# Two chained transformer blocks: the memory layer in two stages with one coefficient table, and a third weight slot for the experts

## The chip, the cores and the metric

One core of one Trainium2 chip runs the whole program in one launch. The metric is device microseconds (us) from the first to the last instruction of a run; lower is better. All data are 32-bit floats.

## The reference, cut to what matters

The program is one block of a first kind, then one of a second kind, on 512 tokens of width 1024. Two parts matter here. The first block ends in a mixture of experts: each token picks 2 of 32 experts, each with three weight matrices.

```python
def expert_block(args):
    xb, e = args
    hid = jax.nn.silu(xb @ w_gate[e]) * (xb @ w_up[e])
    return hid @ w_down[e]
```

The second block has a large memory of 16384 entries (128 x 128 keys), each with a row u and a row v of 1024 numbers. Each token ranks the keys under 8 heads, takes 16 entries per head (128 in all), and sums their v rows, each weighted by its gate and by the gelu of the token's product with u.

```python
v1, i1 = lax.top_k(s1, PEER_TOPK)
v2, i2 = lax.top_k(s2, PEER_TOPK)
...
top, pos = lax.top_k(cand, PEER_TOPK)
...
a = jax.nn.gelu(jnp.einsum('td,thkd->thk', xc, u_tab[ec]), approximate=False)
return jnp.einsum('thk,thkd->td', gc * a, v_tab[ec])
```

## The kernel before, in words

Each stage is a block of five instruction streams (SP and POOL issue DMAs, PE multiplies matrices, ACT and DVE do the rest), written out by hand and tied by semaphores; all engines meet at a stage's end. Weights of ordinary products stream through a ring of two 2 MB halves, `wring`, filled on SP's queue up to two blocks ahead (`load_blocks`, L114).

**Experts** (`stage_router` L1184, `stage_experts` L1358). The router ranks the tokens and builds the row lists. Its SP stream loads eight small tables, then fills the result table `y_dram` in DRAM with 12.6 MB (L1219), because the experts later scatter only used rows into it. The experts run as 24 blocks; a block holds 2 experts of 64 rows each. Of every 6 expert places, 4 are fixed experts and 2 are overflow places, loaded only when used (`cond`, L1432). A block needs 4 MB of gate and up weights (`ex_gu`, two slots) and 2 MB of down weights (`ex_dn`, two slots). On PE the order is: gate and up of block b+1 (L1483), transposes of the hidden rows of b (L1490), transposes of the rows of b+2 (L1473), down of b (L1501). A gate and up slot is refilled when the block two before has used it.

**Retention core** (`stage_ret_core` L942). Its first work on every engine is a decay product on DVE (L986) that waits for two tables, `rc_kdec` and `rc_band`, loaded at the head of its SP stream (L969, L970); PE's first product (L1044) waits for it.

**Memory** (`stage_memory_route` L2037, `stage_memory` L2283). Tokens 256 to 511 (two tiles of 128) are done densely: for each of the 128 blocks of 128 entries, PE multiplies the block of u (0.5 MB) with the tokens, ACT takes the gelu (scores), DVE multiplies by the tokens' coefficients for that block (`weigh`, L2496), and PE multiplies by the block of v (0.5 MB) (outputs, L2394). The coefficients come from one-hot matrices: for 8 tokens DVE compares twice and multiplies once (L2482, L2484, L2487), PE multiplies the two matrices (L2386), and ACT keeps the result (L2445). The table is built in 4 parts of 32 columns, so each group of 8 tokens is done 4 times. Tokens 0 to 255 are done by gathers: POOL issues one indirect DMA per token tile and slot (128 rows of 4 KB, 0.5 MB) into a ring of 8; DVE makes one product and sum per u gather (L2509) and one multiply and add per v gather (L2563).

The route stage ranks 4 token tiles on DVE (47 us each) while PE does the queries, the key scores and the first 32 of the 128 score blocks, whose gelu goes to DRAM (`g_dram`); one of the ranking's products is on POOL (L2092). The memory stage then has a build of the first part of the coefficients (with the u gathers of tile 0 beside it) and four passes of 32 blocks. In the passes stand beside the outputs: the rest of the u gathers of tile 0 and the build of part 2; the v gathers of tile 0, scores, and the build of part 3; the u gathers of tile 1, scores, and part 4; the v gathers of tile 1 and scores.

Of the kernel before, what the change touches and what calls it, by code (L numbers as in the profile page):

```python
# [11 lines left out]

# [38 lines left out]
class Env:  # L51


    def __init__(self, nc, ctx, dram):
# [7 lines left out]
        self.shared = {}  # L62
        self.chained = 0

# [49 lines left out]
def load_blocks(env, sp, ahead=2, until=None):  # L114

    nc = env.nc
    for b in range(env.issued, min(env.used + ahead, len(env.blocks)) if until is None else until):
# [24 lines left out]
class Group:  # L142
# [5 lines left out]
    def __call__(self, eng, steps):  # L148
# [3 lines left out]
        eng.wait_ge(self.sem, self.env.chained)  # L152
# [789 lines left out]
def stage_ret_core(env, R, oT):  # L942
# [9 lines left out]
    with ExitStack() as stk:  # L952
# [226 lines left out]
TRIPLES = LATER // 2  # L1179
UNUSED = 8192.0  # L1180
# [3 lines left out]
def stage_router(env, E):  # L1184
# [6 lines left out]
    with ExitStack() as st:  # L1191
# [19 lines left out]
        with nc.Block() as block:  # L1211
            @block.sync
            def _(sp):
# [3 lines left out]
                for dst, name in loads:  # L1217
                    nc.sync.dma_start(dst[:], dram[name]).then_inc(in_s, 16)
                nc.sync.dma_start(dram["y_dram"].rearrange("(b p) d -> p b d", p=P),  # L1219
                                  env.gates[:, 0, :].unsqueeze(1).broadcast_to([P, NB, D])).then_inc(E.y_set, 16)  # L1220
# [137 lines left out]
def stage_experts(env, E):  # L1358
# [7 lines left out]
    x_got, gu_got, dn_got, y_out = ([env.sem(f"ex_{n}{s}") for s in range(SLOT)]  # L1366
                                    for n in ("x_got", "gu_got", "dn_got", "y_out"))
    gain, shift = (lambda j: env.gain[:, 2, j:j + 1]), (lambda j: env.ada[:, 24 + j, 0:1])
    ROWS, GU, HID, DOWN = [0, 1], [2, 3], 5, [6, 7]
    with ExitStack() as st:  # L1370
# [5 lines left out]
        gu, dn = T("gu", [P, SLOT, 2, GUW]), T("dn", [P, SLOT, 2, EFT * D])  # L1376
        silu, hid, hidT = T("silu", [P, SLOT, EF]), T("hid", [P, SLOT, EF]), T("hidT", [P, SLOT, EFT, P])
        wg = [[gu[:, s, h, :].rearrange("p (k n) -> p k n", k=KD) for h in range(2)] for s in range(SLOT)]
        wd = [[dn[:, s, h, :].rearrange("p (k n) -> p k n", k=EFT) for h in range(2)] for s in range(SLOT)]
# [6 lines left out]
        with nc.Block() as block:  # L1386
            @block.gpsimd
            def _(pool):
# [22 lines left out]
                pool.wait_ge(E.y_set, 16)  # L1411
# [12 lines left out]
            def _(sp):  # L1424
# [3 lines left out]
                def load(part, who, lo, n, s, got, rows=None):  # L1428
                    for h in range(2):
                        src = dram["experts"][bass.ds(who[h], 1), :, lo:lo + n].rearrange("o p n -> p (o n)")  # L1430
                        if rows is not None and rows[h] is not None:
                            nc.sync.dma_start(part[:, s, h, :], src, cond=rows[h]).then_inc(got[s], 16)  # L1432
                        else:
                            nc.sync.dma_start(part[:, s, h, :], src).then_inc(got[s], 16)

                def replace(g, n):

                    b = 3 * g + n
# [1473 lines left out]
```

## Time and profile before

| | us |
|---|---|
| median of 3 runs (3399.39 to 3406.08) | 3400.16 |
| the profiled execution, its own time | 3413.92 |
| its span, first to last instruction | 3412.1 |
| experts, first gate and up product to last down product | 1133.3 to 1483.2 |
| route stage and memory stage, first rank to last gather product | 1993.9 to 3319.8 |

Busy shares of the span: PE 89%, PEld (weight loads) 53%, DVE 47%, ACT 15%, POOL 22%. TensorE's granted clock averages 0.916 of full speed. Traffic is 668.5 MB, of which 281 MB are gathers and scatters. A span's time in a window is read as busy microseconds per engine; a DMA share near 1 means that the 16 DMA engines had packets all the time.

### The profile page before, as it was taken

Reading aid. Unit: us, or ns where it says so; the run is one execution under the profiler, and the core shown is the slowest. Engines: PE = TensorE matmul, PEld = TensorE weight load, DVE = VectorE, ACT = ScalarE, POOL = GpSimd, SP = SyncE. Lnnn points to the kernel's source line nnn. Section 1 sums busy time; section 2 is a strip of 40 time slices with the busy share of each in tenths; the row PEclk is TensorE's granted clock in tenths of the full one; section 3 lists DMA queues with packets and bytes.
Section 4 is the critical chain, followed back from the end, with each engine's and each line's share of the span. In section 5 each row is a group of like instructions: output and inputs, shape, how many; then the busy total and the mean of one; then the engine's idle time right before and its main releaser. Section 6 shows DMA issues by size and latency. Waiting matters only on the chain. (4 is left out here: it accounts for less than half of the span.)

```text
span 3412.1 us, 35969 instructions
## 1 busy us (share of the span) xinstructions
PE 3021.8 (89%) x11616; PEld 1798.3 (53%) x11616; DVE 1616.1 (47%) x3314; ACT 504.0 (15%) x1079; POOL 758.9 (22%) x688
## 2 busy tenths in 40 slices
PE   6988999988986688859888899598899999999987
PEld 3436444445434223324445487495567777776553
DVE  1135100113012212232056169988888888886772
ACT  2223100011001011131146121010000000000002
POOL 0000000000000111110000001345565556556650
PEclk8898998999997799979999899658899999999998
DMA  5010341020115888841200125358999999999992
GB/s 202 37 51 1 148 153 66 35 96 25 74 74 226 344 346 326 318 154 57 105 13 1 50 70 160 132 154 299 326 351 381 366 344 382 362 361 377 410 359 102
DMA packets 156365, 668.54 MB, mean 196 GB/s; under 512 B 22131, under 2 KB 31731, under 8 KB 140915
## 3 DMA queue, kind: packets, MB, share of 16 engines
q1 hardware_dynamic: 73684, 383.16, 29.5%
q0 software_dynamic: 81792, 281.07, 22.2%
q10 hardware_dynamic: 800, 3.15, 0.2%
q8 instruction: 53, 0.87, 0.1%
q14 instruction: 36, 0.29, 0.0%
HBM read 689.31 MB, written 35.65 MB: 212 GB/s over the span
## 5 line engine op out<-in xcount | busy, mean ns | idle before, releaser
L2394 PE MATMUL ps<-wring,pm_weighted 128*128 128x512 f32 x1024 | 488.5, 622 | 41.5 <-DVE pm_weighted L2496 41.4
L414 PE MATMUL ps<-hT,wring 128*128 128x512 f32 (+2 forms) x1232 | 467.3, 541 | 16.4 <-PEq L573 4.9
L414 PEld LDWEIGHTS ps<-hT,wring 128*128 128x128 f32 (+1 forms) x1232 | 233.6, 191 | 247.0 <-issue 238.8
L2368 POOL DMA_INDIRECT pm_ring<-in_peer_u,pm_idxs x256 | 316.4, 1236 | 195.8 <-DVE pm_dots L2509 116.0
L2377 PE MATMUL ps<-hT,wring 128*128 128x256 f32 x1536 | 352.7, 383 | 0.0
L2563 DVE SCALAR_TENSOR_TENSOR gates<-pm_ring,pm_coefs,gates 128x1024 f32<-128x1024 f32 x256 | 316.7, 1280 | 61.1 <-DMA pm_ring<-in_peer_v,pm_idxs 60.9
L2368 POOL DMA_INDIRECT pm_ring<-in_peer_v,pm_idxs x256 | 303.3, 1185 | 139.0 <-issue 57.1
L2394 PEld LDWEIGHTS ps<-wring,pm_weighted 128*128 128x128 f32 x1024 | 197.8, 198 | 255.5 <-issue 196.9
L2386 PEld LDWEIGHTS ps<-pm_onehot,hT 128*128 128x128 f32 x2048 | 294.0, 226 | 49.5 <-issue 49.5
L2377 PEld LDWEIGHTS ps<-hT,wring 128*128 128x128 f32 x1536 | 286.8, 190 | 49.4 <-issue 14.4
L2509 DVE CUSTOM_DVE_ANT_0 pm_ring<-pm_ring,mem_x 128x1024 f32<-128x1024 f32 x256 | 300.5, 1219 | 2.3 <-DMA pm_ring<-in_peer_u,pm_idxs 2.3
L1393 POOL COPY ex_idx<-row_token 128x1 uint32 (+1 forms) x24 | 4.4, 185 | 1304.5 <-PEq L1506 1116.7
L2386 PE MATMUL ps<-pm_onehot,hT 128*128 128x32 f32 x2048 | 286.7, 302 | 2.1 <-DVE pm_onehot L2487 2.1
L1483 PE MATMUL ps<-ex_gu,hT 128*64 128x512 f32 x768 | 187.1, 644 | 49.5 <-DMA ex_gu<-in_experts 47.5
L937 PE MATMUL ps<-wring,hT 128*128 128x512 f32 (+1 forms) x544 | 213.9, 555 | 1.2 <-PEq L362 1.2
L1562 DVE TENSOR_SCALAR hT<-ps,gain,ada 128x128 f32<-128x128 f32 x192 | 63.4, 401 | 278.4 <-PE ps L1473 278.4
L2092 POOL TENSOR_TENSOR pk_eq<-pk_eq,pk_ixf 128x2048 f32<-128x2048 f32 x4 | 26.0, 6488 | 647.2 <-DVE pk_eq L2086 647.2
L937 PEld LDWEIGHTS ps<-wring,hT 128*128 128x128 f32 x544 | 98.4, 190 | 116.2 <-issue 116.2
L2484 DVE TENSOR_TENSOR hT<-pm_iota,pm_keyT 128x1024 f32<-128x1024 f32 x128 | 155.9, 1218 | 0.0
L1483 PEld LDWEIGHTS ps<-ex_gu,hT 128*64 128x64 f32 x768 | 58.7, 148 | 175.7 <-issue 172.2
L2445 ACT ACTIVATE pm_coef_part<-ps 128x256 f32 x128 | 49.2, 384 | 623.8 <-PE ps L2386 623.8
L2496 DVE TENSOR_TENSOR pm_weighted<-pm_weighted,pm_coef_part 128x256 f32<-128x256 f32 x128 | 76.6, 598 | 122.3 <-ACT pm_weighted L2439 82.9
(422 smaller groups left out, 3147.1 us busy)
## 6 DMA issues: line engine op xcount, KB each, us to landing
ex_gu<-in_experts SPq DMA_DIRECT2D x48, 2048.0 KB
wring<-in_peer_v SPq DMA_DIRECT2D x128, 512.0 KB, 7.6
ex_dn<-in_experts SPq DMA_DIRECT2D x48, 1024.0 KB
wring<-in_peer_uT SPq DMA_DIRECT2D x96, 512.0 KB, 5.6
wring<-in_w_in SPq DMA_DIRECT2D x21, 2048.0 KB, 7.7
ada_w<-in_w_ada SPq DMA_DIRECT2D x12, 2048.0 KB, 10.9
pk_u<-in_peer_uT SPq DMA_DIRECT2D x32, 512.0 KB, 3.8
y_dram_out<-gates SPq DMA_DIRECT2D x1, 12288.0 KB, 33.6
```

Source lines behind the costliest of these rows:

```text
L414: mm = env.nc.tensor.matmul(out, w[:, k, lo:hi], rhs(k), start=(k == 0), stop=(k == KD - 1))
L937: mm = env.nc.tensor.matmul(env.ps[:, t[0], 0:n], env.hT[:, k, i * P:(i + 1) * P], w[:, k, lo:lo + n], start=(k == 0), stop=(k == KD - 1))
L1483: mm = nc.tensor.matmul(env.ps[r, GU[s], :], xT[:, s, k, r], wg[s][h][:, k, :], start=(k == 0), stop=(k == KD - 1))
L1562: nc.vector.tensor_scalar(xT[:, s, k, :], env.ps[:, ROWS[n], j * P:(j + 1) * P], gain(k), shift(k), ALU.mult, ALU.add).then_inc(xT_done, 1)
L2368: nc.gpsimd.indirect_dma_start(ring[:, r, :], None, dram[table], bass.IndirectOffsetOnAxis(ap=idx[:, half, r:r + 1], axis=0)).then_inc(got ...
L2377: mm = nc.tensor.matmul(env.ps[:, SCORE[s % 2], 0:DS], uT[s][:, k * P:(k + 1) * P], env.hT[:, k, GT * P:S], start=(k == 0), stop=(k == KD ...
L2386: mm = nc.tensor.matmul(env.ps[:, CB[s % 2], j * PB:(j + 1) * PB], A(s % 2)[:, j, :], B[:, s % 2, j, :], start=True, stop=True)
L2394: mm = nc.tensor.matmul(env.ps[:, OUT[n], :], W[:, s % 2, t * P:(t + 1) * P], vr[s][:, half * WBLK:(half + 1) * WBLK], start=False, stop=stop)
L2484: nc.vector.tensor_tensor(A(s % 2), iota[:].unsqueeze(1).broadcast_to([P, GRP, PK]), keyT[:, 0, ts].unsqueeze(2).broadcast_to([P, GRP, PK] ...
L2496: nc.vector.tensor_tensor(W[:, s % 2, :], W[:, s % 2, :], C[:, part % 2, :, bass.ds(n, 1)].rearrange("p t o -> p (t o)"), ALU.mult).then_i ...
L2509: nc.vector.tensor_tensor_reduce(ring[:, r, :], ring[:, r, :], xg[:, t, :], 1.0, 0.0, ALU.mult, ALU.add, dots[:, n:n + 1]).then_inc(used, 1)
L2563: nc.vector.scalar_tensor_tensor(acc[:, n % 2, :], ring[:, r, :], coef[:, bass.ds(i * PER + n, 1)], acc[:, n % 2, :], ALU.mult, ALU.add).t ...
```

## The change: what it does

1. **Memory, first stage** (`stage_memory_scores`): all 128 score blocks move here, loaded four at a time (2 MB, three buffers: one own, two in `wring`) and stored four at a time. The u gathers of both tiles move here too: as soon as tile 0 is ranked, POOL issues them, and DVE does two products (`FILL`) after the last instruction of each group of the ranking, before it waits for the group. The rest follow after the ranking. The one product that POOL did goes to DVE.
2. **Memory, second stage** (`stage_memory_outputs`): first one table of coefficients `C` [128, 256 tokens, 128 columns] is built on chip, 32 groups of 8 tokens once each, 128 columns wide. Then 128 output blocks, with v in pairs (1 MB), the stored gelu in fours (0.5 MB), and two v gathers a block; the products of the gathers are added straight into `h`. Until the table is done only 3 of the 8 gather buffers are used.
3. **Experts**: a third gate and up slot in `wring`. The weights of the experts that are fixed are loaded in the router stage already: all of block 0, one half of block 1, and one gate and up half of block 2. `wring` is refilled for the second block after the last expert product only.
4. The 12.6 MB fill of `y_dram` moves from the router stage to the head of the retention core's SP stream, ahead of `rc_kdec` and `rc_band`.

```diff
@@ stage_ret_core
             @block.sync
             def _(sp):
+                nc.sync.dma_start(env.dram["y_dram"].rearrange("(b p) d -> p b d", p=P),
+                                  env.gates[:, 0, :].unsqueeze(1).broadcast_to([P, NB, D])).then_inc(env.y_set, 16)
                 nc.sync.dma_start(kdec[:], dram["ret_kdec"]).then_inc(in_s, 16)
@@ stage_router
-                nc.sync.dma_start(env.dram["y_dram"]...).then_inc(E.y_set, 16)
+                for h in range(2):
+                    nc.sync.dma_start(E.gu[0][h], dram["experts"][h, :, 0:GUW]).then_inc(E.gu_got[0], 16)
+                for h in range(2):
+                    nc.sync.dma_start(E.dn[0][h], dram["experts"][h, :, GUW:]).then_inc(E.dn_got[0], 16)
+                for n, h in ((1, 0), (2, 1)):
+                    nc.sync.dma_start(E.gu[n][h], dram["experts"][n + 1, :, 0:GUW]).then_inc(E.gu_got[n], 16)
+                    if n == 1:
+                        nc.sync.dma_start(E.dn[n][h], dram["experts"][n + 1, :, GUW:]).then_inc(E.dn_got[n], 16)
@@ stage_experts, SP
+                def gate_up(i, n):
+                    sp.wait_ge(gu_full, ROUND * i + n - GUS + 1)
+                    load(i, n, E.gu, 0, GUW, gu_got)
+                def down(i, n):
+                    sp.wait_ge(dn_full, 2 * (ROUND * i + n - SLOT) + 2)
+                    load(i, n, E.dn, GUW, GUW + EFT * D, dn_got)
...
@@ stage_memory_scores
+                for n in range(GT * SLOTS):
+                    if n % SLOTS == 0:
+                        pool.wait_ge(rows_s, n // SLOTS + 1)
+                    if n >= RING:
+                        pool.wait_ge(G.used, n - RING + 1)
+                    nc.gpsimd.indirect_dma_start(ring[:, n % RING, :], None, dram["peer_u"], ...)
+                for n in range(QUADS):
+                    if n >= UBUF:
+                        product_done(env, sp, u_t[QUAD * (n - UBUF) + QUAD - 1])
+                    nc.sync.dma_start(u[n % UBUF], dram["peer_uT"][n]).then_inc(u_in[n % UBUF], 16)
+                    if n >= UBUF:
+                        store(n - UBUF)
@@ stage_memory_outputs, DVE
+                with v.Fori(0, groups // 2) as i:
+                    for q in range(2):
+                        v.wait_ge(c_full, n + 1)
+                        nc.vector.tensor_tensor(B[q], iota..., keyT[:, 1, ts]..., ALU.is_equal)
+                        nc.vector.tensor_tensor(A[q], iota..., keyT[:, 0, ts]..., ALU.is_equal)
+                        nc.vector.tensor_tensor(B[q], B[q], keyT[:, 2, ts]..., ALU.mult)
+                v.wait_ge(c_done, 4 + 2 * groups)
+                        for j in range(QUAD):
+                            nc.vector.tensor_tensor(here, here, C[:, :, bass.ds(m, 1)]..., ALU.mult)
+                            for r in (2 * j, 2 * j + 1):
+                                nc.vector.scalar_tensor_tensor(env.h[:, t, :], ring[r], coef..., env.h[:, t, :],
+                                                               ALU.mult, ALU.add)
```

## Rows read from the trace of the kernel before

**Rows 1.** The page, DMA in 40 slices: share of 16 engines, then GB/s

```profile
DMA  5010341020115888841200125358999999999992
GB/s 202 37 51 1 148 153 66 35 96 25 74 74 226 344 346 326 318 154 57 105 13 1 50 70 160 132 154 299 326 351 381 366 344 382 362 361 377 410 359 102
```

**Rows 2.** Windows of the memory: length, busy us by engine, granted clock, DMA share, GB/s

```profile
1990.00:2045.00 55.00, 55.00 (x315) 48.56 (x315) 50.35 (x240) 14.68 (x29) 6.49 (x1) 1.00 0.19 50
2188.00:2300.00 112.00, 109.86 (x515) 107.49 (x513) 97.43 (x164) 12.23 (x33) 63.28 (x43) 0.53 0.61 193
2529.00:2793.00 264.00, 264.00 (x1215) 192.40 (x1213) 225.06 (x251) 23.07 (x60) 157.86 (x140) 1.00 0.98 367
3110.00:3318.00 208.00, 194.59 (x651) 121.30 (x650) 151.90 (x140) 10.38 (x27) 137.78 (x119) 1.00 1.01 405
```

**Rows 3.** Groups by line, memory and route: busy us, mean ns | idle before

```profile
L2394 PE MATMUL ps<-wring,pm_weighted 128*128 128x512 f32 x1024 | 488.5, 622 | 41.5 <-DVE pm_weighted L2496 41.4
L2563 DVE SCALAR_TENSOR_TENSOR gates<-pm_ring,pm_coefs,gates 128x1024 f32<-128x1024 f32 x256 | 316.7, 1280 | 61.1 <-DMA pm_ring<-in_peer_v,pm_idxs 60.9
L2484 DVE TENSOR_TENSOR hT<-pm_iota,pm_keyT 128x1024 f32<-128x1024 f32 x128 | 155.9, 1218 | 0.0
L414 PE MATMUL ps<-hT,pk_u 128*128 128x256 f32 x512 | 113.7, 385 | 7.9 <-DMA pk_u<-in_peer_uT 7.9
L2496 DVE TENSOR_TENSOR pm_weighted<-pm_weighted,pm_coef_part 128x256 f32<-128x256 f32 x128 | 76.6, 598 | 122.3 <-ACT pm_weighted L2439 82.9 <-DMA wring<-in_peer_v 29.8 <-ACT pm_coef_part L2445 8.8
L2487 DVE TENSOR_TENSOR pm_onehot<-pm_onehot,pm_keyT 128x256 f32<-128x256 f32 x128 | 53.4, 417 | 0.0
```

**Rows 4.** Timeline of DVE around the first ranked tile, then a u-gather product

```profile
1993.93 3.20 DVE L2232 MAX8 pk_v<-pk_sc 128x8 f32<-128x128 f32 x16 [26.02 <-ACT pk_sc L2177]
2029.35 6.49 DVE L2092 TENSOR_TENSOR pk_eq<-pk_eq,pk_ixf 128x2048 f32<-128x2048 f32 x1
2040.72 0.23 DVE L2275 CAST mem_rows<-pk_pick 128x128 uint32<-128x128 f32 x1
2195.67 1.22 DVE L2509 CUSTOM_DVE_ANT_0 pm_ring<-pm_ring,mem_x 128x1024 f32<-128x1024 f32 x1
2196.82 0.42 DVE L2482 TENSOR_TENSOR pm_onehot<-pm_iota,pm_keyT 128x256 f32<-128x256 f32 x1
```

**Rows 5.** Timeline of PE in the experts, from a period of three blocks

```profile
1406.57 1.04 PE L1473 MATMUL ps<-ident,hT 128*128 128x128 f32 x8
1411.02 7.04 PE L1483 MATMUL ps<-ex_gu,hT 128*64 128x512 f32 x32
1423.56 7.09 PE L1483 MATMUL ps<-ex_gu,hT 128*64 128x512 f32 x32 [0.67 <-DMA ex_gu<-in_experts]
```

**Rows 6.** Experts: first products (timeline), their group, one period (window)

```profile
1129.35 1.97 PE L1473 MATMUL ps<-ident,hT 128*128 128x128 f32 x8 [14.39 <-DMA hT<-xn_dram_out,ex_idx]
1133.28 9.60 PE L1483 MATMUL ps<-ex_gu,hT 128*64 128x512 f32 x32 [1.97 <-DVE hT L1562]
...
L1483 PE MATMUL ps<-ex_gu,hT 128*64 128x512 f32 x768 | 187.1, 644 | 49.5 <-DMA ex_gu<-in_experts 47.5 <-DVE hT L1562 2.0
...
1397.60:1440.70 43.10, 37.20 (x174) 13.66 (x174) 8.90 (x27) 5.82 (x12) 7.28 (x12) 0.94 0.84 321
```

**Rows 7.** Retention core: SP's issues, PE's first product, the first table's landing

```profile
592.67 130.79 SPq L120 DMA_DIRECT2D wring<-in_w_in  x4
723.99 0.33 SPq L969 DMA_DIRECT2D rc_kdec<-in_ret_kdec  x1
735.90 8.70 PE L1044 MATMUL ps<-ret_v,rc_kd 128*128 128x256 f32 x32 [12.79 <-DVE rc_kd L986]
...
DMA to landing us min/median/max: 7.2/7.2/7.2
```

**Rows 8.** DMA issues of the whole run: KB each, median us to landing

```profile
y_dram_out<-gates SPq DMA_DIRECT2D x1, 12288.0 KB, 33.6
rc_band<-in_ret_band SPq DMA_DIRECT2D x1, 1792.0 KB, 11.0
```

More of the change, by code:

```diff
@@ L151, in __call__ @@
             self.env.chained += 1
-        eng.wait_ge(self.sem, self.env.chained)
+        now = self.env.chained
+        if then is not None:
+            for _ in range(FILL):
+                then()
+        eng.wait_ge(self.sem, now)
 def col(env, name, j=0, n=1):
@@ new lines, in _ @@
+                nc.sync.dma_start(E.gu[1][1], over[:, 0:GUW]).then_inc(gu_got[1], 16)
+                nc.sync.dma_start(E.dn[1][1], over[:, GUW:]).then_inc(dn_got[1], 16)
+                over = dram["experts"][bass.ds(expert(4), 1)].rearrange("o p n -> p (o n)")
+                used = nc.sync.value_load(E.later_used[0:1, 0:1], min_val=0, max_val=1)
+                nc.sync.dma_start(E.gu[2][0], over[:, 0:GUW], cond=used).then_inc(gu_got[2], 16)
+                for n in range(GUS, ROUND):
+                    gate_up(0, n)
+                    down(0, n - 1)
@@ L1462, in _ @@
+                with sp.Fori(1, NB // ROUND) as i:
+                    for n in range(ROUND):
+                        gate_up(i, n)
+                        if n:
+                            down(i, n - 1)
+                        else:
+                            down(i - 1, ROUND - 1)
+                down(NB // ROUND - 1, ROUND - 1)
+                sp.wait_ge(gu_full, NB)
+                env.hold = False
                 load_blocks(env, sp)
@@ L2372, in _ @@
+                gathers(0, first=True)
+                with pool.Fori(1, GT * SLOTS // (2 * RING)) as i:
+                    gathers(i)
             @block.tensor
             def _(pe):
-                def scores(turn, s):
-                    pe.wait_ge(table_got[s], table0 + 32 * turn + 32)
-                    for k in range(KD):
-                        mm = nc.tensor.matmul(env.ps[:, SCORE[s % 2], 0:DS], uT[s][:, k * P:(k + 1) * P],
-                                              env.hT[:, k, GT * P:S], start=(k == 0), stop=(k == KD - 1))
-                    mm.then_inc(score_full, 1)
@@ L2417, in _ @@
-                scores(TURNS, 0)
-                for part in range(1, PARTS - 1):
-                    with pe.Fori(0, TURNS) as i:
-                        for s in range(STEP):
-                            scores(*after(part * TURNS + i, s))
-                            outputs(part * TURNS + i, s)
-                            coefficients(part + 1, i, s)
-                with pe.Fori((PARTS - 1) * TURNS, PARTS * TURNS - 1) as turn:
-                    for s in range(STEP):
-                        scores(*after(turn, s))
-                        outputs(turn, s)
@@ L2433, in _ @@
+                with pe.Fori(0, QUADS // 2 - 1) as i:
+                    outputs(i)
+                outputs(QUADS // 2 - 1, last=True)
             @block.scalar
             def _(act):
[L2435 to L2439 removed]
```

682 lines of the change are left out of this document (310 added, 372 removed).

## The prediction

> **What bounds the kernel now.** I read the page first, then windows over the memory, the groups by line, and timelines of the three places that the change touches. In the page's DMA lines [rows 1] the reader is to see two long stretches of full DMA (slices 14 to 17, the experts, and 28 to 39, the memory) with half-idle slices between and ahead of them. The windows [rows 2] say which engine bounds a pass of the memory. In the pass of 2529 to 2793 PE is busy 264.00 of 264.00 us: it does scores, outputs and a part of the coefficients, and DMA moves 367 GB/s. In the last pass, without coefficients, PE has gaps and DMA moves 405 GB/s at a share of 1.01: that pass is DMA-bound, 3.15 MB a block (6 times 0.524) in 7.75 us. Ahead of them, 1990 to 2045 moves 50 GB/s and 2188 to 2300 only 193, with DVE the busiest engine. So two resources take turns, PE (coefficients done 4 times) and DMA, and neither is used in the ranking. The change evens this out.
>
> In the experts PE waits 47.5 us in all for gate and up weights, and a period of three blocks is 43.1 us at 321 GB/s [rows 6]. The retention core starts 12.79 us late on a table that came 7.2 us after its issue [rows 7].
>
> **The sum, part by part.** It is made against the profiled execution (3413.92 us, span 3412.1), which is 13.8 us above the median of 3400.16; I take the same saving off the median. Two runs of this kernel can be told apart at about 0.2% (7 us).
>
> *Memory, first stage.* The first tile is ranked from 1993.93 to 2040.95 [rows 4], as before; its product L2092 took 6.49 us beside the one on POOL, and now there are two alone, like the other 2048-wide operations some 2.3 us each, so 1.9 us less, which I leave out. From then on three engines race. DMA: 128 blocks of u (67.1 MB), the stored gelu (16.8 MB) and 256 gathers (134.2 MB) are 218.1 MB; three fours (6.3 MB) are in by then, so 211.8 MB remain, 523 us at 405 GB/s [rows 2]. DVE: three more tiles at 47.0 us less 1.9, and 256 products at 1.15 us start to start [rows 4] plus 0.1, is 135 + 320 = 455 us. PE: score blocks at 113.7 / 32 = 3.55 us [rows 3], 454 us from about 2024. So DMA ends last, near 2564. POOL was busy 157.86 us with the 128 gathers of the second window [rows 2], 1.2 us each, 315 us for 256, covered. The waits inside the ranking (two gather products behind each group) delay only the ranking, which has over 60 us to spare; ACT can sit behind an exponential for tile 3 and hold PE for some 10 us, which the buffers and the same slack cover.
>
> *Memory, second stage.* About 4 us of start (gelu of the coefficients, transposes already done). The table: 32 groups, three DVE operations 1024 wide, 1.22 us each [rows 3], 1.14 start to start, 3.4 to 3.7 us a group, 109 to 117 us. PE needs 16 passes of 128 columns a group: 8 such passes took 1.97 us at half clock [rows 6] and 1.04 at full [rows 5], so 3.9 or 2.1 us; at half clock PE would set the end, 126 us. The old build ran at a granted clock of 0.53 [rows 2]. I take 118. Nothing hides it: the gathers stop at 3 buffers, so DMA brings only 4.7 MB ahead.
> Outputs: a block is 0.524 MB of v, 0.131 of gelu and two gathers, 1.70 MB, 218.1 MB less 4.7 in all, 213.4 / 0.405 = 527 us, 4.1 us a block. PE has 488.5 / 128 = 3.8 us a block and DVE 0.60 + 2 x 1.28 = 3.2 [rows 3]; both fit under it, PE closely. One price is not in the trace: `weigh` now reads the table with a step of 512 bytes, before 128. At 128 bytes it takes 598 ns against 417 for the same shape without a step [rows 3]. Bounds: no more than now (598), or in step with the distance (4 times the 181 ns extra, 1.14 us, block 3.7 us). I take 598; either end is under 4.1.
> The Trainium skill ("SBUF — State Buffer", the note on cachelines) says that each access that leaves a 16-byte line pays, so it would give 598 ns at both steps, and the sum would not change.
> End: 2564 + 4 + 118 + 527 = 3213, and the old last gather product ended at 3319.8. **Memory -106 us.** If the two DMA-bound stages ran only at the 367 GB/s of the PE-bound pass, they would be 54 + 55 us longer.
>
> *Experts.* A block costs PE 1423.56 - 1411.02 - 0.67 = 11.87 us when nothing waits [rows 5], 24 of them 285. The slots ask 4 fixed experts and the rows, 321 x 43.1 = 13.8 MB a period, 34.2 us at 405 GB/s; so DMA and PE (35.6) are level, and I take 36.5 a period in place of 43.1: -53 us over 8. In front, 11.5 MB are loaded in the router, on a DMA that before did the fill there; the first gather then doesn't share the DMA with 12 MB of weights, and the first product comes 5 us earlier than 1133.28 [rows 6]. **-58 us**; between -10 (the two down slots or DMA keep 43 us) and -70 (PE alone). The late refill of `wring` (4 MB, 10 us at the end of the experts) is hidden by the last down products and the sum of the experts: without that cover it costs 10.
>
> *The fill, moved.* In the router it was off the path, so taking it away brings nothing by itself. At the new place it is issued first on SP, at 723.99, and the tables come behind it. That a queue keeps its order shows here: an 8 KB table took 7.2 us to land, behind a 2 MB block issued just before, and the 1.8 MB table 11.0 [rows 7, 8], which is what 3.9 MB need at 405 GB/s. The fill took 33.6 us to land [rows 8], 2 of it latency: **+31 us** of waiting for DVE, and PE behind it; every engine of the stage waits for that first product. Bounds 0 (the tables pass the fill) and 34.
>
> Sum: -106 - 58 + 31 = -133 us: 3281 in the profiled execution's terms, **3267 us** against the median.
>
> **The rivals.**
> *R1, a weaker pace of DMA (0.12).* Loads in twos and fours wait for whole groups, and gathers for a ring of 8; if this keeps the mean at the 367 GB/s of the second window [rows 2], the memory gives back 109 us: 3376. For: slots are refilled in larger units than now. Against: in the last pass the same mix ran at 405 with four slots.
> *R2, a lower ceiling (0.04).* If two streams of reads, stores and gathers together are held to 358 GB/s for the whole of both stages, they take 592 + 596 in place of 523 + 527 us, +138: 3405, no change. Against: 208 us at 405 [rows 2].
> The Trainium skill ("DMA: Bandwidth & Descriptors", Bandwidth) gives about 358 GB/s as one core's share of HBM when both of a pair stream; by that rule R2 would hold, and the trace's 405 disagrees for this core.
> *R3, the tables pass the fill (0.10).* No 31 us: 3236. Against it is the 7.2 us of an 8 KB table [rows 7].
> *R4, the third slot does nothing (0.12).* If the bound is the two down slots or DMA itself, the period stays 43: experts -8, 3317. Against: the wait that the rows show is for `ex_gu` [rows 5, 6].
> *R5, slower (0.04).* DVE becomes the bound of the outputs through `weigh`'s 512-byte step. It decides above 4.1 - 2.56 = 1.5 us an operation, and the change is a loss above 1.5 + 133 / 128 = 2.6 us, 4.3 times today's. At 3 us a block takes 5.56, the outputs 712: +185, 3452. For: no row shows this step. Against: 128 bytes cost only 181 ns for 256 elements.
> Forecast: 0.58.
>
> **How the numbers follow.** The forecast's own range is 3225 to 3310: table 109 to 126, experts -35 to -70, DMA 395 to 412 GB/s. To hold 8 in 10 I add R3 (3236) and R4 (3317) and leave out R1, R2 and R5, together 0.20: 3215 to 3345. Faster by over 0.2%: forecast, R1, R3, R4, 0.92; R2 lies on the edge and is split, so within 0.2% 0.02, slower 0.06 with R5 and the tail of R2.
>
> **What would show each step.** In the profile of the changed kernel: PE's first product of the retention core waits some 44 us, not 12.8, on the decay product, behind `rc_kdec` or `rc_band`. PE's waits for `ex_gu` shrink from 47.5 us to under 15, and three blocks take 35 to 38 us. The first memory stage shows about 405 GB/s from the first ranked tile to its end, with u-gather products waiting for DMA; 3.4 to 4 us between one-hot groups; then outputs at 4.1 us a block with DVE and PE both waiting for DMA. The forecast is wrong if output blocks take over 4.4 us, if `weigh` takes over 1.5 us, or if a window of the first stage has DVE or PE without gaps while DMA is under 380 GB/s.

## The result, and the profile after

The changed kernel takes **3282.65 us** (median of 4 runs, 3279.74 to 3285.75) beside 3400.93 us for the kernel before on the same chip: a ratio of 0.965, 95% interval 0.9633 to 0.9667. The profiled execution took 3285.16 us (span 3283.3), the one of before 3413.92 (span 3412.1).

Cut at the same instructions, the two spans compare so (us; the experts and the outputs from first to last product or operation, by their starts):

| stretch | before | after | difference | forecast |
|---|---|---|---|---|
| start to the retention core's first product | 735.9 | 765.8 | +29.9 | +31 |
| from there to the first gate and up product | 397.4 | 399.4 | +2.0 | -5 |
| experts, to the last down product | 349.3 | 288.1 | -61.2 | -53 |
| to the first ranking of the memory | 511.3 | 512.2 | +0.9 | 0 |
| memory, to the end of its products | 1325.9 | 1225.0 | -100.9 | -106 |
| tail | 92.3 | 92.8 | +0.5 | 0 |

The page's DMA lines of the changed kernel, 40 slices each, against [rows 1]:

```profile
DMA  5100251123022479971210026999999249999992
GB/s 201 48 30 24 103 204 59 51 98 155 26 77 77 171 320 409 391 300 72 77 65 7 1 84 243 416 402 346 419 416 372 81 193 413 413 414 413 413 363 86
```

Two stretches of full DMA, the first of 346 to 419 GB/s and the second of 413, stand where the memory of before swung between 299 and 410. The hole of a slice and a half between them is the coefficient table. The windows of the memory stages show it closer (length, busy us of PE, PEld, DVE, ACT and POOL, granted clock, DMA share, GB/s), against [rows 2]:

```profile
2012.00:2255.00 243.00, 242.73 (x1161) 213.46 (x1160) 209.22 (x723) 39.16 (x84) 129.50 (x101) 1.00 1.01 402
2255.00:2285.00 30.00, 15.81 (x74) 13.57 (x72) 30.00 (x136) 1.96 (x4) 18.92 (x14) 0.81 0.78 272
2285.00:2465.00 180.00, 176.61 (x806) 154.67 (x806) 120.26 (x195) 20.27 (x56) 99.57 (x87) 0.98 1.01 413
2465.00:2551.20 86.20, 0.00 (x0) 0.00 (x0) 75.20 (x122) 1.75 (x4) 62.35 (x55) 0.50 0.95 364
2554.00:2666.00 112.00, 69.86 (x519) 61.16 (x518) 109.09 (x96) 34.01 (x63) 3.92 (x3) 0.99 0.10 42
2667.00:3190.00 523.00, 462.47 (x1020) 185.03 (x1021) 382.00 (x384) 0.00 (x0) 351.80 (x284) 1.00 1.01 408
```

Ranking, scores and u gathers run at 402 to 413 GB/s, with two weak places: 30 us at 272, and the last 86 us, in which TensorE has nothing left and the gathers run alone at 364. The table is DVE's alone, 109.09 of 112 us busy, 42 GB/s beside it. The outputs hold 408 GB/s from end to end. The groups by line (busy us, mean ns, idle before and what ended it), against [rows 3, 6]:

```profile
L1514 PE MATMUL ps<-ex_gu,hT 128*64 128x512 f32 x512 | 115.8, 606 | 5.5 <-DVE hT L1603 4.3 <-DMA ex_gu<-in_experts 1.3
L1514 PE MATMUL ps<-wring,hT 128*64 128x512 f32 x256 | 56.3, 592 | 0.0
L2468 PE MATMUL ps<-pm_v_rows,pm_weighted 128*128 128x512 f32 x1024 | 464.7, 603 | 62.0 <-DVE pm_weighted L2518 44.3 <-DMA pm_v_rows<-in_peer_v 17.7
L428 PE MATMUL ps<-hT,wring 128*128 128x256 f32 x1664 | 365.4, 381 | 17.7 <-ACT pk_g L2249 14.4 <-DMA pk_iota<-in_iota 3.4
L2285 DVE CUSTOM_DVE_ANT_0 pk_ring<-pk_ring,mem_x 128x1024 f32<-128x1024 f32 x256 | 309.7, 1224 | 104.5 <-DMA pk_ring<-in_peer_u,pk_rows 99.6 <-issue 0.5
L2518 DVE TENSOR_TENSOR pm_weighted<-pm_weighted,pm_coef_table 128x256 f32<-128x256 f32 x128 | 75.7, 591 | 3.7 <-ACT pm_coef_table L2486 3.7
```

TensorE's wait on `ex_gu` is 1.3 us, from 47.5 (the third slot lies in `wring`, second row, without a wait). The multiply with the step of 512 bytes takes 591 ns, the bound of 598 taken and not 1.14 us. The stall of 14.4 us of TensorE on ACT is new. Last, the retention core: TensorE's first product in the timeline, and the two DMA issues with KB and us to landing, against [rows 7, 8]:

```profile
765.77 10.22 PE L1060 MATMUL ps<-ret_v,rc_kd 128*128 128x256 f32 x32 [43.84 <-DVE rc_kd L1002]
...
y_dram_out<-gates SPq DMA_DIRECT2D x1, 12288.0 KB, 38.1
rc_kdec<-in_ret_kdec SPq DMA_DIRECT2D x1, 8.0 KB, 37.8
```

The issue of that table on SP (first row, duration in ns), and what ended DVE's idle time ahead of its decay product:

```profile
L985 SPq DMA_DIRECT2D rc_kdec<-in_ret_kdec x1: 23890/23890/23890, 723.3 to 723.3; - x1
  DMA rc_band<-in_ret_band: 115.5, 1
```

The 8 KB table lands 37.8 us after its issue where it took 7.2. The issue itself lasts 23.9 us on SP, 0.33 before, so the second table, `rc_band`, goes out only at 747.2, lands 18.0 us later at 765.2, and it is this one that ends DVE's wait. Both tables stand behind the fill, and the retention core starts 30 us late. The Trainium skill ("DMA: Bandwidth & Descriptors", Two DMAs through the same engine are not ordered) says that descriptors of one queue of a DMA engine start in order; this row agrees: the fill lands at 760.9, the table at 761.1.

### The profile page after: what moved, and what is told of

It reads as the page before. It is cut to its first block and busy times, and to the rows that moved or that the text cites. A ratio compares the mean times of both kernels' runs of the same rounds, so it can differ in the third digit from the quotient of the medians.

```text
span 3283.3 us, 30222 instructions
## 1 busy us (share of the span) xinstructions
PE 2788.1 (85%) x10080; PEld 1561.4 (48%) x10080; DVE 1478.0 (45%) x3007; ACT 490.4 (15%) x1015; POOL 734.7 (22%) x652
## 5 line engine op out<-in xcount | busy, mean ns | idle before, releaser
L428 PE MATMUL ps<-hT,wring 128*128 128x256 f32 (+1 forms) x2576 | 763.3, 458 | 30.3 <-ACT pk_g L2249 14.4
L428 PEld LDWEIGHTS ps<-hT,wring 128*128 128x128 f32 x2576 | 491.1, 191 | 297.3 <-issue 253.5
L2468 PE MATMUL ps<-pm_v_rows,pm_weighted 128*128 128x512 f32 x1024 | 464.7, 603 | 62.0 <-DVE pm_weighted L2518 44.3
L2143 POOL DMA_INDIRECT pk_ring<-in_peer_u,pk_rows x256 | 311.3, 1216 | 760.6 <-DVEq L2357 537.0
L2285 DVE CUSTOM_DVE_ANT_0 pk_ring<-pk_ring,mem_x 128x1024 f32<-128x1024 f32 x256 | 309.7, 1224 | 104.5 <-DMA pk_ring<-in_peer_u,pk_rows 99.6
L2468 PEld LDWEIGHTS ps<-pm_v_rows,pm_weighted 128*128 128x128 f32 x1024 | 185.7, 189 | 340.4 <-issue 227.6
L2436 POOL DMA_INDIRECT hT<-in_peer_v,pm_idxs x192 | 251.7, 1311 | 211.5 <-PE ps L2456 107.8
L2524 DVE SCALAR_TENSOR_TENSOR h_tok<-hT,gates,h_tok 128x1024 f32<-128x1024 f32 x192 | 244.6, 1282 | 100.3 <-DMA hT<-in_peer_v,pm_idxs 65.0
L428 PE MATMUL ps<-hT,pk_u 128*128 128x256 f32 x704 | 153.8, 379 | 0.0
L428 PEld LDWEIGHTS ps<-hT,pk_u 128*128 128x128 f32 x704 | 133.7, 190 | 18.3
```

What stands on the lines that cost most here:

```text
L428: mm = env.nc.tensor.matmul(out, w[:, k, lo:hi], rhs(k), start=(k == 0), stop=(k == KD - 1))
L2143: nc.gpsimd.indirect_dma_start(ring[:, n % RING, :], None, dram["peer_u"], bass.IndirectOffsetOnAxis(ap=rows[:, n // SLOTS, n % SLOTS:n % ...
L2285: V.tensor_tensor_reduce(ring[:, r, :], ring[:, r, :], xg[:, t, :], 1.0, 0.0, ALU.mult, ALU.add, G.coef[:, t, n % SLOTS:n % SLOTS + 1]).th ...
L2436: nc.gpsimd.indirect_dma_start(ring[r], None, dram["peer_v"], bass.IndirectOffsetOnAxis(ap=idx[:, half, r:r + 1], axis=0)).then_inc(got[r] ...
L2468: mm = nc.tensor.matmul(env.ps[:, OUT[n], :], W[q][:, j * DS + t * P:j * DS + (t + 1) * P], vr[j // 2][:, j % 2 * D + half * WBLK:j % 2 * ...
L2524: nc.vector.scalar_tensor_tensor(env.h[:, t, :], ring[r], coef[:, t, bass.ds(RING * i + n // GT, 1)], env.h[:, t, :], ALU.mult, ALU.add).t ...
```

## The experiments

E1 to E4 ran on one chip, E5 to E8 on another, E9 to E12 on a third; the kernel before took 3409.62, 3400.68 and 3406.10 us (medians) there. What a stage takes is read from the traces, by the starts of the same instructions as in the table above.

**E4, the changed kernel again,** so that E1 to E3 have it beside them.

> The changed kernel itself, unedited, on the chip of the three others, so that they can be compared with it there: 3283 us within 3, rc_kdec again some 38 us from issue to landing, TensorE's wait of 14 us on ACT again in the ranking stage. If one of these does not come back, it is a chance of one execution and not a consequence of the order of the work.

Measured: 3274.31 us (3272.57 to 3282.53), ratio 0.9614 (0.9596 to 0.9633), span 3271.8; the table landed after 37.8 us, TensorE waited 13.8 us on ACT. The total is 8 us lower than on the first chip, where the kernel before was 9 us faster than here; no run explains that, and it limits what medians across chips can say. Both effects come back, so they belong to the order of the work. The first memory stage took 580.3 us from the first ranking to the end of the last gather product (585.6 in the first profile): an execution differs from another by that much.

**E1, the fill behind the core's loads.**

```
-                nc.sync.dma_start(env.dram["y_dram"]..., <gates, broadcast>).then_inc(env.y_set, 16)
...
                     nc.sync.dma_start(qdec[:, hd % 2], row).then_inc(qdec_in[hd % 2], 16)
+                nc.sync.dma_start(env.dram["y_dram"]..., <gates, broadcast>).then_inc(env.y_set, 16)
```

> Edit: the 12.6 MB fill of y_dram is issued at the end of the retention core's loads on SP, behind the last qdec row, instead of ahead of the rc_kdec table. Theory A (the table stood behind the fill in the same issuing queue, and what matters is that small loads lie behind it): rc_kdec lands some 7 us after its issue instead of 37.8, the first product of the retention core waits 13 us instead of 43.8 and starts near 736 instead of 766, everything after it is 31 us earlier, span 3252, because the product loop that follows asks for little DMA. Rival B (the fill costs its 33 us of DMA time wherever it is put, since it then stands ahead of the weights that the next stage loads): the 31 us move to a wait later in the retention core or at the branches, span within 5 us of 3283. Between them: a part of it, if the branches' first weights are late by 10 to 20 us.

Measured: 3245.44 us, ratio 0.9525 (0.9509 to 0.9541), apart from E4's interval; span 3242.8, **-29.0 us**. The same lines as above, of E1:

```profile
734.66 8.74 PE L1060 MATMUL ps<-ret_v,rc_kd 128*128 128x256 f32 x32 [12.70 <-DVE rc_kd L1002]
...
y_dram_out<-gates SPq DMA_DIRECT2D x1, 12288.0 KB, 34.9
rc_kdec<-in_ret_kdec SPq DMA_DIRECT2D x1, 8.0 KB, 7.1
```

From the first product to the experts it is 396.6 us, with 396.4 in E4: the fill costs nothing there. Theory A holds; what cost 31 us was two tables, of 8 KB and 1.8 MB, behind 12.6 MB.

**E3, the first token gather ahead of the experts' next weights.**

```
+                sp.wait_ge(x_got[0], 16)
                 over = dram["experts"][bass.ds(expert(3), 1)]...
```

> Edit: SP waits for the first gather of tokens to land before it issues the expert weight loads that follow the prefetched ones. Theory A (the first gather of tokens shares the DMA engines with those weights, and is late by that): the first product of the experts, which waits 13.1 us for it, starts 5 us earlier, and nothing is late behind it; span 3278. Rival B (the 13 us are the latency of a gather that reads what has just been written, which no other traffic lengthens): the wait stays 13 us, span 3283 within 2. Rival C (the weights that now start later become the wait): the first product starts earlier and the third to fifth block waits for its gate and up weights, span 3283 to 3290.

Measured: 3270.28 us, ratio 0.9597 (0.9581 to 0.9613), which overlaps E4's; span 3267.8. Here the trace is sharper than the total. TensorE's first transposes of the experts, of E3:

```profile
1153.79 1.97 PE L1505 MATMUL ps<-ident,hT 128*128 128x128 f32 x8 [7.92 <-DMA hT<-xn_dram_out,ex_idx]
```

The wait is 7.92 us, where it was 13.1, and the stretch from the retention core to the experts 391.2 us with 396.4 (391.3 to 391.7 in the three later kernels that have this line). The experts themselves take 287.0. Theory A: **-5 us**.

**E2, the third tile's exponential later on ACT.** In the changed kernel ACT reaches `exponentials(3)` four groups after the second tile's and sits there. E2's edit:

```
-                table(TABLE[2], TABLE[2] + 4)
+                table(TABLE[2], TABLE[2] + 16)
                 exponentials(3)
```

> Edit: in the ranking stage ACT takes the exponential of the third tile's table twelve groups later, so that the products and copies of the u side don't stand behind it. Theory A (the exponential, waiting 38 us for DVE's ranking of that tile, holds ACT's evictions, they hold TensorE, TensorE stops freeing the buffers of the gathers, and the DMA queues run dry at 272 GB/s for 30 us): the wait of 14.4 us of TensorE on ACT goes, the stretch from 2255 to 2285 runs at 400 GB/s or over, and the stage ends 8 to 10 us earlier, span 3274. Rival B (the gathers are bound by DVE's ranking and POOL's issues there, and TensorE's stall only uses slack): the stall goes and the time does not, span 3283 within 3. Rival C (the exponential comes at the end of the stage and the coefficient table starts later by its 4 to 5 us): span 3283 to 3288.

Measured: 3273.31 us, ratio 0.9605 (0.9589 to 0.9621), not to be told from E4; span 3266.8. ACT's exponentials of the changed kernel (first row) and of E2 (second) in the timeline:

```profile
2283.01 0.31 ACT L2241 ACTIVATE pk_ex<-pk_ex 128x128 f32<-128x128 f32 x1 [38.05 <-DVE pk_ex L2331]
```

```profile
2281.60 0.31 ACT L2241 ACTIVATE pk_ex<-pk_ex 128x128 f32<-128x128 f32 x1
```

The stall is gone, and TensorE's with it. The windows of E2 that answer to those above:

```profile
2247.00:2277.00 30.00, 30.00 (x141) 26.41 (x140) 29.66 (x139) 3.45 (x9) 17.92 (x14) 1.00 0.98 369
...
2300.00:2457.00 157.00, 139.32 (x649) 122.44 (x647) 114.11 (x177) 16.69 (x43) 90.46 (x81) 0.96 1.02 416
2457.00:2536.00 79.00, 0.00 (x0) 0.00 (x0) 70.57 (x116) 0.00 (x0) 54.68 (x51) 0.50 0.95 365
```

The 30 us move 369 GB/s in place of 272 (270 in E4), but TensorE is then through its score blocks earlier (near 2300 + 139 = 2439, in E4 near 2451), and the gathers run alone for 97 us, not 88. The stage took 574.5 us here, but 580.9 in E8 and 577.6 in E12 with the same edit, and 578.6 to 581.3 in six kernels with the stall (E1, E3 to E7; 585.6 in the first profile). The means differ by some 3 us, but the stage of one and the same kernel differs by 5 from one execution to another, so no gain is shown; the 8 to 10 us of theory A can be ruled out. Most of what the stall loses comes back at the end.

**E5, two slots with the early loads kept.**

```
-GUS = 3
+GUS = 2
-                for n, h in ((1, 0), (2, 1)):
+                for n, h in ((1, 0),):
```

> Edit: two slots for the experts' gate and up weights instead of three, everything else as changed; the early loads under the router are kept but for the half of the third block, which has no slot any more. Theory A (the third slot carries the gain of the experts: it lets a weight transfer run while TensorE works on two blocks): the period of three blocks goes back from 35.1 to some 41 to 43 us, TensorE's wait on ex_gu from 1.2 to over 30 us, first gate and up product to last down product from 288 to 330 to 345 us, span 3271.8 + 45 = 3317. Rival B (the early loads carry the gain, since they take three of the weight transfers out of the stage): first to last product stays under 300 us, span 3272 to 3285. The start of the experts is the same in both, 1161 us.

Measured: 3283.43 us, ratio 0.965 (0.9613 to 0.9686), span 3279.3. Experts 294.8 us with 287.7 in E4, TensorE's wait on `ex_gu` 5.4 us. **My theory A fell**: the third slot is worth 7 us. The numbers are rival B's, but its reason is not proved by that, as the next two show.

**E6, three slots without the early loads,** and **E7, the memory's change alone.** E6 moves the seven static weight loads from the router's SP block to the start of the experts' block. E7 does this too, with `GUS = 2` and with the fill back in the router.

> Edit: the third slot is kept, but the weight loads that the change issues under the router are issued on SP at the start of the experts instead, as before the change. Theory A (the third slot carries the gain of the steady period, the early loads only that of the first blocks): first to last product 288 + 10 to 15 = 300 us, with the wait in the first two blocks and the period of three blocks still 35.1 us from the third pair on, span 3284. Rival B (with three slots and nothing prefetched the loads never catch up, since three blocks' weights take about as long on the DMA engines as three blocks' products): the period stays over 37 us and first to last product takes 320 us or more, span over 3300. Rival C (the loads at the start are hidden by the token gather's wait): within 4 us of 3272.

> Edit: the memory's two stages alone; the experts have two slots, their loads all start in the stage, and the fill of y_dram is back under the router. Theory A (the three parts add up: the memory gives 101 to 106, the experts 61, the moved fill takes 31): span 3412.1 - 101 = 3311 beside a profiled run of before, and 3274.3 + 61 - 31 = 3304 beside the changed kernel on this chip; first product of the retention core after a wait of 13 us and 7 us for rc_kdec; from the first gate and up product to the last down product 350 us. Rival B (the parts don't add, since a memory stage that starts at another time or clock is another stage): the memory stages take over 5 us more or less than the 1215 us from first ranking to the end of the products of the changed kernel.

Measured: E6 3290.92 us, ratio 0.9668 (0.9631 to 0.9704), span 3294.9, experts 298.8 us, of which TensorE waited 13.3 for `ex_gu`, 11.5 of it ahead of the second block; theory A of E6 holds for the stage; the span is 11 us over its number, 7 of them ahead of the experts (first gate and up product at 1167.6, in E4 at 1160.8). E7 **3259.75 us**, ratio 0.9583 (0.9547 to 0.962), span 3257.4: 14 us less in span than the whole change in E4 on another chip, where I had expected 30 more. The memory was as expected (1217.8 us from the first ranking to the last multiply of the outputs, 1218.3 in E4), the retention core too (12.7 us of wait). But the experts took 298.9 us, with neither third slot nor early loads, where the kernel before takes 349.3. Something else in the changed experts gives 50 us.

**What it was.** One thing that all these kernels share is the order in which SP issues. SP's issues and TensorE's products in the timeline of the kernel **before**:

```profile
1325.43 0.33 SPq L1434 DMA_DIRECT2D ex_dn<-in_experts  x1
1326.05 0.08 SPq L1432 DMA_DIRECT2D ex_dn<-in_experts  x1
1328.51 0.08 SPq L1432 DMA_DIRECT2D ex_gu<-in_experts  x1
1328.79 0.34 SPq L1434 DMA_DIRECT2D ex_gu<-in_experts  x1
...
1313.30 7.09 PE L1483 MATMUL ps<-ex_gu,hT 128*64 128x512 f32 x32 [2.74 <-DMA ex_gu<-in_experts]
1321.56 3.65 PE L1501 MATMUL ps<-ex_dn,ex_hidT 128*64 128x512 f32 x16
1325.04 7.04 PE L1483 MATMUL ps<-ex_gu,hT 128*64 128x512 f32 x32
1338.71 1.51 PE L1483 MATMUL ps<-ex_gu,hT 128*64 128x512 f32 x6 [1.80 <-DMA ex_gu<-in_experts]
```

The gate and up product ends at 1313.30 + 7.09 = 1320.39 and its slot is free. Its next load goes out only at 1328.51, 8.1 us later (L1432 is the conditional issue for a place of the overflow, L1434 the other half's, at 1328.79). SP stands at the wait for the down product that ends at 1325.2, 4.8 of the 8.1 us. Then it issues the down load and reads the numbers of the next block's experts, the other 3.3 us, and only then comes to the gate and up load. It is so in every block of the middle: 7.4 to 8.5 us from the fourth block on. The product that uses the load waits at 1338.71.

**E9, the kernel before with the changed order alone.**

```
                 for n in range(6):
-                    replace(2 * i, n)              # gu(b), then dn(b)
+                    replace(2 * i, n, "gu")        # gu(b), then dn(b - 1)
+                    replace(2 * i, n - 1, "dn")    # of the round before, for n = 0
```

> Edit: the kernel before with one thing of the change's experts alone. SP issues the gate and up load of block b, then the down load of block b - 1, where before it issued the gate and up load of b and then the down load of b. Two slots each, all loads in the stage, the memory as before. Theory A (in the old order SP stands at the wait for the down product of block b - 2 while the gate and up slot of block b + 1 is already free; the load of b + 1 goes out only when that down product is done, some 4.5 us later each time): the experts' first to last product falls from 349.9 to 299 us as in the kernel with the memory's change alone, TensorE's wait on ex_gu from 47.5 to 10 us, the period of three blocks from 43.1 to 35 to 36, span 3412 - 51 = 3361. Rival B (the order of the two loads is nothing, and the gain of the kernel with the memory alone came from something else of the changed experts, such as reading the expert's number behind the wait or the state in which the stage finds the DMA): 345 to 350 us, span 3412 within 5.

Measured: 3351.38 us, ratio 0.9821 (0.9782 to 0.986), span 3353.9. Experts 299.9 us: **-49.4 us** by the order of two issues. The same lines of E9:

```profile
1307.57 0.86 SPq L1434 DMA_DIRECT2D ex_gu<-in_experts  x2
1312.53 0.08 SPq L1432 DMA_DIRECT2D ex_dn<-in_experts  x1
1319.26 0.33 SPq L1434 DMA_DIRECT2D ex_gu<-in_experts  x1
...
1300.30 7.04 PE L1492 MATMUL ps<-ex_gu,hT 128*64 128x512 f32 x32
1308.51 3.65 PE L1510 MATMUL ps<-ex_dn,ex_hidT 128*64 128x512 f32 x16
1311.99 7.04 PE L1492 MATMUL ps<-ex_gu,hT 128*64 128x512 f32 x32
1323.68 1.89 PE L1492 MATMUL ps<-ex_gu,hT 128*64 128x512 f32 x8
```

The product ends at 1307.34 and the load leaves at 1307.57, 0.2 us later; its use at 1323.68 does not wait. The swap takes both parts of the 8.1 us away, since SP now reads the numbers while it would wait anyway; how much of the 49.4 us each part is worth was not tried apart.

**E10, the changed kernel with the old order,** three slots and early loads kept.

```
-                        gate_up(i, n)
                         down(i, n - 1)             # or the round before's last
+                        gate_up(i, n)
```

> Edit: the changed kernel with its third slot and its early loads, but with the old order of SP's loads in the experts: the down load of block b goes out ahead of the gate and up load of b + 1. Theory A (order): the gate and up load again leaves only when the down product of block b - 2 is done, 11.7 us of TensorE's work ahead of its use as in the kernel before, whether there are two slots or three; so the third slot does nothing, the period of three blocks is 41 to 43 us, first to last product 335 to 345 us, span 3272 + 50 = 3322. Rival B (the third slot gives the lead by itself): first to last product under 300 us, span under 3285.

Measured: 3349.98 us, ratio 0.9829 (0.9796 to 0.9862), span 3347.6, experts **361.9 us**. Theory A, by more than its number. The groups of the gate and up products, of E9 and of E10:

```profile
L1492 PE MATMUL ps<-ex_gu,hT 128*64 128x512 f32 x768 | 175.0, 609 | 14.1 <-DMA ex_gu<-in_experts 12.1 <-DVE hT L1571 2.0
```

```profile
L1514 PE MATMUL ps<-ex_gu,hT 128*64 128x512 f32 x512 | 126.6, 652 | 40.5 <-DMA ex_gu<-in_experts 36.2 <-DVE hT L1603 4.3
L1514 PE MATMUL ps<-wring,hT 128*64 128x512 f32 x256 | 65.0, 666 | 17.2 <-DMA wring<-in_experts 17.2
```

With three slots and the old order TensorE waits 36.2 + 17.2 us, more than the 47.5 of before with two. Why more is argued, not tried: the changed code reads the expert's number behind the wait, where before it was read ahead of it. From the down product's end to the next gate and up load SP takes 3.1 to 4.4 us in E10 and 2.5 to 3.7 before. The down load of before leaves 0.2 us after its product (1325.21, 1325.43), that of E10 1.7 us after (1324.18, 1325.90; TensorE's down product stands at 1320.53 for 3.65 us).

```profile
1325.90 0.08 SPq L1460 DMA_DIRECT2D ex_dn<-in_experts  x1
...
1320.53 3.65 PE L1533 MATMUL ps<-ex_dn,ex_hidT 128*64 128x512 f32 x16
```

Together, the experts by starts, in us:

| order | slots | early loads | us | kernel |
|---|---|---|---|---|
| old | 2 | no | 349.3 | before |
| old | 3 | yes | 361.9 | E10 |
| new | 2 | no | 299.9, 298.9 | E9, E7 |
| new | 3 | no | 298.8 | E6 |
| new | 2 | yes | 294.8 | E5 |
| new | 3 | yes | 287.7, 288.1 | E4, after |

E6 and E7 look as if the third slot did nothing, but two things cancel there. E6 issues the third block's first 2 MB ahead of the second half of the second block's weights, so its second block starts 22.0 us after the first, in E7 16.6. From there to the last down product E6 takes 276.8 us and E7 282.2. With the early loads the same stretch is 274.4 us (E4) and 281.6 (E5). So in the new order the third slot is worth 5 to 7 us behind the second block.

The changed kernel's loads leave late as well, 8.4 to 9.1 us after their slot is free from the fifth block on. The load for the third slot, and its uses before and behind it:

```profile
1314.05 0.33 SPq L1462 DMA_DIRECT2D wring<-in_experts  x1
...
1297.30 7.04 PE L1514 MATMUL ps<-wring,hT 128*64 128x512 f32 x32
1332.38 7.04 PE L1514 MATMUL ps<-wring,hT 128*64 128x512 f32 x32
```

It costs nothing there, since the load leaves 18.3 us ahead of its use. In E9 it is 15.6 to 16.1 us from the thirteenth block on, and in the kernel before it is 8.4 to 9.9 us for every third block from the ninth on. What counts is this lead, not the delay behind the free slot alone.

**E8, all three mends:** E1, E2 and E3 in one kernel.

> Edit: the fill behind the retention core's loads, the exponential of the third tile twelve groups later, and the wait for the first token gather ahead of the experts' later weight loads, together. Theory A (they sit in three stages and add up): the spans of the three single edits against the changed kernel on the same chip were -29.0, -5.0 and -4.0, so span 3234 and median 3237, a ratio of 0.950 to before. Rival B (with the fill later, less of the exponential's or the gather's gain is left, because neither showed beyond the scatter in the medians): median 3243 to 3246.

Measured: **3236.57 us** (median of 6, 3232.35 to 3246.56), ratio 0.9507 (0.9479 to 0.9534). Theory A's median. Its profiled run was the slowest of the six (span 3244.7), so its stages say more than its total: 391.3 us from the retention core to the experts, 287.0 in them, but 580.9 in the first memory stage. The fill and the gather add up; the exponential shows nothing.

**E11, three gather products in place of two behind each ranking group,** and **E12, two buffers for score blocks,** both on E8.

```
-FILL = 2
+FILL = 3
```

```
-UBUF = 3
+UBUF = 2
```

> Edit: the kernel with all three mends, and three gather products in place of two behind each group of ranking operations on DVE. Theory A (what is left between 575 to 581 us and the 523 us of transfers at 405 GB/s is the end of the stage, where the gathers run alone for 80 us at 361 to 381 GB/s because they were held back under the ranking; more of them under the ranking shorten that end): more gathers are done by the end of the last ranking, the stretch without products of TensorE shrinks to under 60 us, first ranking to last gather product 572 us or less (580.9 in the kernel with the three mends), span 3237. Rival B (the gathers under the ranking are bound by POOL's issues and the DMA, and the ranking is only drawn out): stage 581 within 3 or longer, span 3245 to 3255.

> Edit: the kernel with all three mends, and two buffers of four score blocks in place of three. Theory A (the score blocks' loads take the DMA engines from the gathers; with fewer of them in flight the gathers get on, and the two streams end nearer together): the end without products of TensorE shrinks from 82 us to under 60, stage 572 us or less, span 3237. Rival B (two buffers can't hide a load of four blocks, 5.2 us alone and twice that beside the gathers, behind the 3.45 us of a product, so the DMA falls under 390 GB/s in the mixed stretch): stage 585 to 610 us, span 3250 to 3275. I hold this one likelier.

Measured: E11 3253.87 us, ratio 0.9551 (0.9518 to 0.9584), stage 593.1 us. E12 3237.00 us, ratio 0.9504 (0.947 to 0.9537), stage 577.6 us. Neither theory of E12 holds: two buffers are as good as three, with 100 us of gathers alone at the end, since TensorE did not slow down. E11's span of 3250.0 us and its longer stage are rival B's, whose reason also fits in part: the ranking is drawn out (379 us from its first to its last search for the largest keys, 296 in E8). The end with gathers alone shrinks to 42 us, as theory A wanted, and the stage is longer all the same. A part of the loss is one that I had not named. What engines waited for in E11's stage (us in total, times, longest):

```profile
ACT pk_ex L2241 <- DVE pk_ex L2331: 37.5, 1, 37.5
```

is the changed kernel's row (E4), and E11 has:

```profile
ACT pk_ex L2242 <- DVE pk_ex L2332: 110.0, 2, 95.5
PE ps L428 <- ACT pk_g L2250: 71.8, 1, 71.8
```

The drawn out ranking brings the exponential late again, ACT waits 95.5 us and holds TensorE for 71.8. If all of the 593.1 - 580.9 = 12.2 us is the stall's, which no run shows apart from the third product itself, a microsecond of it costs 0.17. By this estimate the changed kernel's 14.4 us cost 2.4, as much as the means of E2, E8 and E12 differ from the kernels with the stall.

## Why the prediction was right and where it was wrong

The time was inside the range and 15.7 us over the number. Of these, 10.5 are the profiled execution: by its own time the saving is 3413.92 - 3285.16 = 128.8 us, by the medians 118.3. I took the saving off the median unchanged, as if the 13.8 us that this execution stood above its median would be in both profiles; after stood 2.5 above. In the profile's own terms I forecast -133 us and -128.8 came.

- *Memory, -106:* right, -100.9. Outputs 523.5 us for 527, start and table 116 for 122 (3.40 us a group, TensorE at a granted clock of 0.99, DVE the bound). The first stage took 16 us more than forecast. The volume was right (539.2 us at 392 GB/s, 211 MB for 211.8), the pace was not: 30 us at 272 and 86 us at 364 lose 9.9 and 8.7 us against 405, 243 us at 402 lose 1.8, and 180 us at 413 give 3.6 back. The step that failed is "which the buffers and the same slack cover": ACT behind the exponential held TensorE and with it the loads, 30 us at 272 GB/s. But its price is some 2 to 3 us by the estimate above, and not clear of the scatter of the stage. The other part is the end: the sum itself has TensorE done near 2478 and DMA at 2564, so 86 us of gathers alone, and prices them at 405 GB/s; 364 came. What holds them there is open.
- *The fill, +31:* right in mechanism and size, +29.9 at the first product, +31.9 at the experts; E1 gives 29.7 back there beside E4. R3 is out. The queue held the issue as well (23.9 us), which the sum does not name. One reading ahead of it is off: 3.9 MB at 405 GB/s are 9.7 us, not the 11.0 that the 1.8 MB table took.
- *Experts, -58:* right in size (-61.2 in the stage, and with the stretch ahead of it -59.2), **wrong in its reason**, so that the number came by luck. "so DMA and PE (35.6) are level" took for granted that a third slot was what let them be level. The wait was for `ex_gu`, but not for want of a slot: the load left 8.1 us after its slot was free, behind another wait and SP's own reads. The order gives 49.4 us, third slot and early loads together 11.1, of which the third slot is 5 to 7. R4, that the third slot does nothing, was nearer to the truth than the forecast, and its time was false: it left out the order too. The prediction never asks what the two swapped lines do to SP's own wait.
- *First gather 5 us earlier:* wrong, it waited 13.1 us. SP still issues three weight loads, of 2, 1 and 2 MB, at the head of the stage; E3 shows that keeping them back brings the 5 us.
- *R1 and R2:* out, 402 to 413 GB/s where two streams run. The Trainium skill's "HBM Reference" (Specifications) says that a core that streams alone goes well above its share of some 358 GB/s, which is for two cores at once; the outputs' 408 agree.
- *R5:* out, 591 ns.
- *The signs of being wrong:* output blocks took 4.1 us and `weigh` 0.59, as forecast. The third sign did show: from 2255 to 2285 DVE is busy 30.00 of 30 us while DMA moves 272 GB/s. It marks the term that was too small, the first stage.

So the change as made holds a part that costs more than it brings: the early loads and the third slot give 11 us, and the fill's new place takes 31. E7 without either is 14 us shorter in span. With the fill behind the tables both are to be had: E8 and E12 are 37 to 38 us under E4 by medians, on other chips, and by ratio 0.9507 to 0.9614.

## What to carry to other kernels

A queue that waits on several semaphores in turn should meet them in the order in which the other engine reaches them. Before adding a buffer for a load that is late, compare when its slot came free with when the load was issued: if there are microseconds between and the use waits, the issue is held by something else, and a further slot behind the same wait need not help (E10: 361.9 us with three slots, 349.3 before with two). If the use does not wait, the same delay is harmless. And put tables that someone is waiting for ahead of a large transfer in the same queue, not behind it.

## What the runs showed of the hardware that was not expected

- Gathers of 4 KB rows alone move 361 to 386 GB/s here, with 8 buffers, as means over the 79 to 98 us at the end of the stage (E8 361, after 364, E2 365, E4 381, E12 386); beside a stream of blocks the same stage moves 413 to 416. In stretches of 20 us they reach 406 and fall to 325 (after), so the mean is no fixed ceiling, and its cause is open.
- An issue can hold the engine that makes it: SP's issue of the 8 KB table lasted 23.9 us behind the 12.6 MB fill, 0.33 us without it.
- A first gather for which TensorE waits 13.1 us beside three weight loads (5.2 MB) takes 5 us less without them.
- The multiply's step of 512 bytes costs what 128 did, 591 and 598 ns.
- Reading numbers into registers behind a wait delays an issue: 0.2 us from the down product's end before, 1.7 with two reads in E10 (rows above; a read's load is 0.27 us, with register operations around it). It did no harm where the load had slack (E7 with E9).
